# A hybrid decoder block on one core: mixing-gate chunks dealt 2, 2, 2, 10, a third bank for spread decays, routing over 65 candidates with six gather slots

## The chip, the cores and the metric

One Trainium2 chip, one of its cores, one launch. The metric is the device time of the launch in microseconds. The engines are named as in the profile: PE (TensorE, matmul; PEld is its weight load), DVE (VectorE), ACT (ScalarE), POOL (GpSimd) and SP (SyncE, which here only issues DMAs).

## The reference, cut to what matters

512 tokens, width 1024, with 16 meta tokens ahead (528 columns, TOK). One layer:

```python
xn = rms_norm(h, g1); proj = xn @ w_in     # sb q,k,v | dn q,k,v | dn z | b, a | gate_sb, gate_dn
o_sb = stick_breaking_attention(rms_norm(q), rms_norm(k), v)          # 8 heads of 64
o_dn = gated_delta_rule_chunked(l2(silu(conv(dq))), l2(silu(conv(dk))), silu(conv(dv)), beta, g)
o_dn = rms_norm(o_dn) * silu(z)
mix = sigmoid(gate_sb) * (o_sb @ w_sb_out) + sigmoid(gate_dn) * (o_dn @ w_dn_out)
h = h + mix @ w_o
# PEER: 8 heads, 2 x 128 sub keys, top 16 of each half, then top 16 of the 16 x 16 sums
s1, i1 = lax.top_k(s[:, :, 0], 16); s2, i2 = lax.top_k(s[:, :, 1], 16)
cand_s = s1[..., :, None] + s2[..., None, :]
cand_i = i1[..., :, None] * 128 + i2[..., None, :]
top_s, pos = lax.top_k(cand_s, 16); expert_idx = cand_i[pos]; gate = softmax(top_s)
y[t] = sum_e gelu(x[t] . u_tab[expert_idx]) * gate * v_tab[expert_idx]
h = h + y
```

## The kernel before, in words

The kernel has two halves, `front` and `back`. Every float32 product with a large weight is made of three matmuls on a high and a low part (`products`, lines 84 to 86): ACT copies out the high part (`hi`), DVE or POOL subtracts it to get the low one (`lo`, `low`).

**front** computes the projections and both branches, for four pairs of heads one after the other. Its weights come as 40 chunks of 128 columns through a ring of three (`ring`). A chunk is eight steps of TensorE, one for each 128 rows of the contraction: a step of a gate, z or q chunk is three matmuls of 512 columns, one of a k, dq, dk or dv chunk six of 264. Six chunks belong to each pair; the 16 chunks of the two mixing gates (`gate`) belong to none and are dealt out by `GATES_PER_PAIR`, so many to each pair. `Plan` spreads the steps over named places of a pair's program (`room`: "start", "sums", "grow1", "sums2", "grow2" to "grow4", "turned", ("kk", n), "inverse0", ("level", a), ("unit", u), "wt", ("chain", n, s), "end"); a pair's quota is its share of the gates and then the six chunks of the next pair. It also says where a chunk's weights are split and its result taken (`split`, `take`), at most a place or so behind the steps. The projections of pair i+1 so run among the attention and delta-rule work of pair i.

Early in a pair stands the spreading of the decays. For each of five token tiles n (tile 0 is the 16 meta tokens) `grow(n)` on TensorE copies rows of log-decays and betas over all partitions into a PSUM bank (line 1019); DVE's `grow_rows(n)` reads it (800), ACT takes exponentials (592, 595), DVE's `beta_decay(n)` multiplies (808), and POOL masks (439). The banks are `n % 2`, so that `grow(n)` from n = 2 on waits for `beta_decay(n - 2)`. Then come ten transposes (1042 to 1045) into banks 4, 2 and 5, the k k^T products (1053), the blockwise inverse (1063 to 1096), in whose places the attention runs (1107 to 1130), and a chain over the tiles (1139 to 1179) with a norm at its end (1185).

**back** mixes, projects out, makes queries and scores, and then streams the experts: 128 chunks of `activations(j)` (24 matmuls of 384 columns, 3 for each 128 rows) and 128 of `outputs(j)`. In the activations ACT runs `hi(U + s)`, then at set places `exponents(i)` (line 1436, which first waits for DVE's `shifted`), then `gelu(s - 3)`; `activations(j)` waits for `gelu(j - 2)` and for the low part of its own chunk, which POOL makes (line 1520) for j = 3 to PAIRS_A + 2 and DVE after that.

Meanwhile DVE routes (`route(i)`, four tiles of 128 tokens): top 16 of each half, by `best` (MAX8, FIND_INDEX8 and MATCH_REPLACE8), the 16 x 16 sums (line 1672), top 16 of 256 sums in each of 8 heads, and, by comparing positions with 0 to 15 (1688), multiplying (1692) and summing (1697), the two sub keys of each pick. `turn(i)` and `take` bring a tile's picks to columns at chunks ROUTED_AT. The first 128 tokens (FEW) are computed in another way: POOL gathers their experts' rows, one row of 1024 for each token (line 1514), in 128 gathers of u and 128 of v, and DVE multiplies them (`few_next`, "dots", 1721 and 1728). POOL's first R = 4 gathers stand ahead of `low(U + 13)`; after that `sent` grows with j. 78 dots (26 a tile) go with the routing of tiles 1 to 3 in a ring of four slots (`few_ring`), 50 with the gates in two slots (`u_ring`), the v rows in `few_ring` again. `u_ring` shares its memory with the later `w_hi` and `w_lo`, `few_ring` with the one-hot tiles.

From chunk PAIRS_A on, 48 `gates(p)` (two-hot matmuls) follow the activations of one chunk each. The last DVE work ahead of the outputs is the trailing dots and lows. SP loads weights and stores activations in program order (`load_next`, line 1341, waits for the low part of the chunk ahead; `store_acts`, 1349), and after all 128 it loads back what the outputs need (`load_w`, 1360 and 1363); then DVE `weigh`s (1756).

## Time and profile before

| | |
|---|---|
| median of three runs | 2131.11 us (2120.71, 2133.23, 2131.11) |
| the profiled execution's own time | 2122.74 us |
| its span, first to last instruction | 2121.0 us |
| busy: PE, PEld, DVE, ACT, POOL | 1971.5, 1751.7, 1392.6, 815.3, 674.7 us |
| mean of a high part on ACT (1401), a low part on POOL (1520) | 1061 ns, 2575 ns |
| front, to the last norm (line 1185) | 0 to 689 us |
| activations | 901 to 1547 us |
| outputs | 1555 to 2117 us |

The span is one profiled execution, from its first to its last instruction. Busy time counts only what an engine computes. A wait list says for whom an engine waited; in a timeline a row's second number is its duration, and the bracket is the idle time ahead of it with what ended it. A granted clock of 1.00 is 2.4 GHz.

### The profile page before, as it was taken

To read this page: it belongs to the slowest core of one execution; us is meant where nothing else is said; L and a number is where in the kernel's file an instruction comes from. 1 tells how busy PE (TensorE), PEld (TensorE's weight loads), DVE (VectorE), ACT (ScalarE), POOL (GpSimd) and SP (SyncE) were. 2 spreads that over 40 slices of the span, in tenths; PEclk is the share of its full clock that TensorE was granted. 3 is DMA by queue.
4 is the path that set the end of the run, shared out by engine and by line. 5 is a ranking of instruction groups with operands and counts; after the bars stand their busy time and mean duration, and the time that the engine had idled before them with its cause. 6 is when DMAs were issued, how large, how long until landed. Compare 5 with 4: busy or idle time off the path is not lost. (4 is left out here: it accounts for less than half of the span.)

```text
span 2121.0 us, 30502 instructions
## 1 busy us (share of the span) xinstructions
PE 1971.5 (93%) x11569; PEld 1751.7 (83%) x11569; DVE 1392.6 (66%) x2636; ACT 815.3 (38%) x1260; POOL 674.7 (32%) x685
## 2 busy tenths in 40 slices
PE   8889989899898799989999989989989999999999
PEld 7767676676665588889898989989989999999999
DVE  5543443443542564399898968788767777777777
ACT  4333433433433443233333336655523333333332
POOL 4133033033031100058979761222312223222221
PEclk9999999999999899999999999999999999999999
DMA  3210110210210652248888877888889999999997
GB/s 113 85 40 21 55 41 21 69 37 11 70 36 6 225 157 82 80 125 294 289 308 300 296 248 259 323 303 310 304 283 323 325 319 324 326 321 328 325 328 243
DMA packets 153377, 421.75 MB, mean 199 GB/s; under 512 B 15760, under 2 KB 69136, under 8 KB 152592
## 3 DMA queue, kind: packets, MB, share of 16 engines
q1 hardware_dynamic: 114448, 279.27, 38.0%
q0 software_dynamic: 38784, 140.53, 20.0%
q8 instruction: 93, 1.52, 0.3%
q14 instruction: 52, 0.43, 0.1%
HBM read 365.21 MB, written 54.53 MB: 198 GB/s over the span
## 5 line engine op out<-in xcount | busy, mean ns | idle before, releaser
L1401 ACT ACTIVATE expert_hi<-raw 128x1024 fp32r<-128x1024 f32 x288 | 305.4, 1061 | 429.1 <-PE psE L86 394.3
L84 PE MATMUL psE<-x2h,expert_hi 128*128 128x384 f32 x1024 | 353.3, 345 | 28.5 <-POOL expert_lo L1520 20.2
L84 PE MATMUL psE<-w_hi,expert_hi 128*128 128x384 f32 x1024 | 350.7, 342 | 16.4 <-DVE expert_lo L1556 7.5
L1556 DVE TENSOR_TENSOR expert_lo<-raw,expert_hi 128x1024 fp32r<-128x1024 f32 x212 | 259.5, 1225 | 148.7 <-ACT expert_hi L1401 147.8
L86 PE MATMUL psE<-x2h,expert_lo 128*128 128x384 f32 x1024 | 346.9, 339 | 0.0
L85 PE MATMUL psE<-x2l,expert_hi 128*128 128x384 f32 x1024 | 346.8, 339 | 0.0
L86 PE MATMUL psE<-w_hi,expert_lo 128*128 128x384 f32 x1024 | 343.8, 336 | 0.0
L85 PE MATMUL psE<-w_lo,expert_hi 128*128 128x384 f32 x1024 | 343.6, 336 | 0.0
L1514 POOL DMA_INDIRECT few_gathered<-in_peer_v,picked_expert x128 | 135.7, 1060 | 431.1 <-DVE shared L1728 389.7
L1520 POOL TENSOR_TENSOR expert_lo<-raw,expert_hi 128x1024 fp32r<-128x1024 f32 x76 | 195.7, 2575 | 144.5 <-ACT expert_hi L1401 142.9
L84 PEld LDWEIGHTS psE<-w_hi,expert_hi 128*128 128x128 f32 x1024 | 192.6, 188 | 38.3 <-issue 28.0
L84 PEld LDWEIGHTS psE<-x2h,expert_hi 128*128 128x128 f32 x1024 | 196.3, 192 | 33.4 <-POOL expert_lo L1520 24.6
L85 PEld LDWEIGHTS psE<-x2l,expert_hi 128*128 128x128 f32 x1024 | 196.1, 192 | 0.0
L86 PEld LDWEIGHTS psE<-x2h,expert_lo 128*128 128x128 f32 x1024 | 195.7, 191 | 0.0
L85 PEld LDWEIGHTS psE<-w_lo,expert_hi 128*128 128x128 f32 x1024 | 192.8, 188 | 0.0
L86 PEld LDWEIGHTS psE<-w_hi,expert_lo 128*128 128x128 f32 x1024 | 192.7, 188 | 0.0
L1432 ACT ACTIVATE gelu<-psE 128x384 f32<-128x384 f32 x128 | 63.0, 492 | 318.1 <-PE psE L86 318.0
L84 PE MATMUL psB<-xh,ring_h 128*128 128x264 f32 (+1 forms) x448 | 169.0, 377 | 16.2 <-DVE proj L675 12.1
L1728 DVE SCALAR_TENSOR_TENSOR shared<-few_gathered,few_act,shared 128x1024 f32<-128x1024 f32 x127 | 162.5, 1279 | 0.3
L85 PE MATMUL psB<-xl,ring_h 128*128 128x264 f32 (+1 forms) x448 | 152.6, 341 | 0.0
L86 PE MATMUL psB<-xh,ring_l 128*128 128x264 f32 (+1 forms) x448 | 152.0, 339 | 0.0
L881 DVE TENSOR_TENSOR inverse<-inverse,psB 128x512 f32<-128x512 f32 (+3 forms) x108 | 64.1, 594 | 123.8 <-PE psB L1096 123.6
(286 smaller groups left out, 3624.9 us busy)
## 6 DMA issues: line engine op xcount, KB each, us to landing
raw<-in_peer_u SPq DMA_DIRECT2D x128, 512.0 KB, 4.5
raw<-in_peer_v SPq DMA_DIRECT2D x128, 512.0 KB, 6.9
expert_acts<-gelu SPq DMA_DIRECT2D x128, 192.0 KB, 5.1
shared<-expert_acts SPq DMA_DIRECT2D x128, 192.0 KB, 4.0
expert_gates<-shared SPq DMA_DIRECT2D x5, 4096.0 KB, 17.2
shared<-expert_gates SPq DMA_DIRECT2D x32, 640.0 KB, 6.7
ring<-in_w_xonly SPq DMA_DIRECT2D x24, 512.0 KB, 3.4
ring<-in_w_full SPq DMA_DIRECT2D x16, 512.0 KB, 3.8
```

Of the source, the lines that this page charges most:

```text
L84: nc.tensor.matmul(out, sh, mh, start=first, stop=False)
L85: nc.tensor.matmul(out, sh, ml, start=False, stop=False)
L86: return nc.tensor.matmul(out, sl, mh, start=False, stop=last)
L881: inc(nc.vector.tensor_tensor(part, part, bank[0:r, 3 if t % 2 else 5, 0:4 * r].rearrange("p (e w c) -> p e w c", e=2, w=2)[:, :, w0:, :], ...
L1401: nc.scalar.activation(wh[:, s % R, :], raw[:, s % R, :], ACT.Copy).then_inc(S["hi_done"], 1)
L1432: nc.scalar.activation(acts[:, j % R, :], ps[:, 6 + j % 2, 0:MANY], ACT.Gelu).then_inc(S["gelu_done"], 1)
L1514: pool.indirect_dma_start(ring[:, r, :], None, source, bass.IndirectOffsetOnAxis(ap=picked_expert[:, n % HK:n % HK + 1], axis=0)).then_inc ...
L1520: nc.gpsimd.tensor_tensor(wl[:, s % R, :], raw[:, s % R, :], wh[:, s % R, :].bitcast(F32), ALU.subtract).then_inc(S["lo_done"], 1)
L1556: v.tensor_tensor(wl[:, s % R, :], raw[:, s % R, :], wh[:, s % R, :].bitcast(F32), ALU.subtract).then_inc(S["lo_done"], 1)
L1728: last = v.scalar_tensor_tensor(out=few_y, in0=ring[:, r, :], scalar=share, in1=few_y, op0=ALU.mult, op1=ALU.add)
```

## The change

Four things are changed.

1. `GATES_PER_PAIR` is (2, 2, 2, 10) and was (3, 3, 3, 7).
2. `grow(n)` uses banks 0, 1 and 4 in turn and waits for `beta_decay(n - 3)`; the transposes, which write bank 4, wait for `beta_decay` of tile 2.
3. `route` builds 65 sums for each head, in five blocks (`CORNERS`): row 0 with all 16 columns, rows 1 and 2 with 8, 3 to 6 with 4, 7 to 14 with 2, row 15 with 1. A sum that stands in none of them has at least 16 sums that are not smaller. The sub keys are found from a position by 16 start values (`starts`): one comparison (is_ge), a multiplication with the differences of neighbouring rows' index plus start (`corner_step`) and a sum; then by small operations, and by one comparison (is_equal), a multiplication and a sum for the second half.
4. The gathered rows have one ring of 2 + R = 6 slots: all six in the routing, slots 0 and 1 with the gates, 2 to 5 for v. Six gathers stand ahead of `low(U + 13)`. TILE_DOTS is 25 and was 26, ROUTED_AT (13, 33, 53, 73) and was (13, 34, 55, 76), and `exponents(i)` stands one chunk later (s + 3 for s + 4).

```diff
-GATES_PER_PAIR = (3, 3, 3, 7)
+GATES_PER_PAIR = (2, 2, 2, 10)
...
+        def grow_bank(n):
+
+            return (0, 1, 4)[n % 3]
...
-                        decays[0:r, n, :, 0, 0:r], bank[0:r, n % 2, 2 * r:4 * r].rearrange("p (e c) -> p e c", e=2),
+                        decays[0:r, n, :, 0, 0:r], bank[0:r, grow_bank(n), 2 * r:4 * r].rearrange("p (e c) -> p e c", e=2),
...
-                    if n >= 2:
-                        wait("decay_beta", n - 1)
+                    if n >= 3:
+                        wait("decay_beta", n - 2)
...
                 wait("silued", 3)
+                wait("decay_beta", 3)
...
-TILE_DOTS = 26
+TILE_DOTS = 25
...
-ROUTED_AT = (13, 34, 55, 76)
+ROUTED_AT = (13, 33, 53, 73)
+CORNERS = ((0, 1, 16), (1, 2, 8), (3, 4, 4), (7, 8, 2), (15, 1, 1))
+CANDS = sum(a * b for _, a, b in CORNERS)
...
-        def few_seat(n):
...
+        seats, turns, users = [], [0] * (2 + R), {}
+        for n in range(2 * HK):
+
+            r = n % (2 + R) if n < ROUTE_DOTS else (n - ROUTE_DOTS) % 2 if n < FIRST_DOTS else 2 + (n - FIRST_DOTS) % R
+            turns[r] += 1
+            seats.append((r, turns[r], users.get(r, -1) + 1))
+            users[r] = n
...
-                if s + 4 in ROUTED_AT:
-                    exponents(ROUTED_AT.index(s + 4))
+                if s + 3 in ROUTED_AT:
+                    exponents(ROUTED_AT.index(s + 3))
...
-            for n in range(R):
+            for n in range(2 + R):
                 gather(n)
-            sent = R
+            sent = 2 + R
...
-                step(v.tensor_tensor(square(cand), along(val[:, :, 0, :]), across(val[:, :, 1, :]), ALU.add))
+                at_row = 0
+                for a, rows_, cols_ in CORNERS:
+                    part = [P, HEADS, rows_, cols_]
+                    last = v.tensor_tensor(
+                        cand[:, :, at_row:at_row + rows_ * cols_].rearrange("p h (a b) -> p h a b", b=cols_),
+                        val[:, :, 0, a:a + rows_].rearrange("p h (a b) -> p h a b", b=1).broadcast_to(part),
+                        val[:, :, 1, 0:cols_].rearrange("p h (a b) -> p h a b", a=1).broadcast_to(part), ALU.add)
+                    at_row += rows_ * cols_
+                step(last)
...
-                for k in range(2):
-                    last = v.tensor_tensor(square(match[:, k, :, :]), ranks, along(rankf[:, k, :, :]), ALU.is_equal)
-                step(last)
...
+                step(v.tensor_tensor(square(match[:, 0, :, :]), along(posf), small(0), ALU.is_ge))
                 dots_next()
...
+                step(v.tensor_tensor(square(match[:, 0, :, :]), square(match[:, 0, :, :]), across(corner_step),
+                                     ALU.mult))
+                step(v.tensor_reduce(flat(picked[:, 0, :]), square(match[:, 0, :, :]), AX_X, ALU.add))
                 dots_next()
...
+                step(v.tensor_copy(rank[:, 0, :, :], flat(picked[:, 0, :])))
+                step(v.tensor_scalar(rank[:, 1, :, :], rank[:, 0, :, :], KEYS * P - KEYS, None, ALU.bitwise_and))
+                v.tensor_tensor(flat(picked[:, 0, :]), rank[:, 0, :, :], rank[:, 1, :, :], ALU.subtract)
+                step(v.tensor_tensor(posf, posf, rank[:, 1, :, :], ALU.subtract))
+                step(v.tensor_tensor(square(match[:, 1, :, :]), along(posf), small(1), ALU.is_equal))
+                step(v.tensor_tensor(square(match[:, 1, :, :]), square(match[:, 1, :, :]), across(idxf[:, :, 1, :]), ALU.mult))
+                v.tensor_reduce(flat(picked[:, 1, :]), square(match[:, 1, :, :]), AX_X, ALU.add)
                 dots_next()
```

How the steps move on TensorE, in pair 1 and around the spreading: before, nine gate steps stand between the sums of squares and the transposes (4, 3 and 2 of them, three rows each), with a `grow` behind each lot.

```order
L84 MATMUL psB<-xh,ring_h 128x512
L85 MATMUL psB<-xl,ring_h 128x512
L86 MATMUL psB<-xh,ring_l 128x512
...
L1019 MATMUL psB<-rows_in,ones 128x512
L1042 MATMUL psB<-ident,kq 128x128
```

Now one gate step (the last that this pair has), `grow(2)` and `grow(3)` in a row, three steps of the next pair's dq, `grow(4)`, and three dq steps more.

```order
L1016 MATMUL psB<-norm_work,blocks 128x16
L84 MATMUL psB<-xh,ring_h 128x512
L85 MATMUL psB<-xl,ring_h 128x512
L86 MATMUL psB<-xh,ring_l 128x512
L1023 MATMUL psB<-rows_in,ones 128x512 x2
L84 MATMUL psB<-xh,ring_h 128x264
L85 MATMUL psB<-xl,ring_h 128x264
L86 MATMUL psB<-xh,ring_l 128x264
...
L1023 MATMUL psB<-rows_in,ones 128x512
...
L1047 MATMUL psB<-ident,kq 128x128
```

In the whole of such a pair, 2 dq steps (6 before) follow the transposes, then 0, 2, 2, 2, 2 (2, 0, 2, 2, 2 before) the five k k^T products, and none (2) the first transposes of the inverse; from there on nothing is changed in pairs 0 to 2. In pair 3 the counts up to the third cumulated attention tile are as before, and 24 gate steps more stand behind it, at the places of the levels, "unit", "wt" and the first "chain", where pairs 0 to 2 have 24 steps of z, k and q and pair 3 had none.

On POOL, at the head of the activations, before the low part of chunk 13:

```order
L1520 TENSOR_TENSOR expert_lo<-raw,expert_hi 128x1024 x10
L1514 DMA few_gathered<-in_peer_u_rows,picked_expert 128x1024 x4
L1520 TENSOR_TENSOR expert_lo<-raw,expert_hi 128x1024
L1514 DMA few_gathered<-in_peer_u_rows,picked_expert 128x1024
```

and now:

```order
L1524 TENSOR_TENSOR expert_lo<-raw,expert_hi 128x1024 x10
L1518 DMA few_gathered<-in_peer_u_rows,picked_expert 128x1024 x6
L1524 TENSOR_TENSOR expert_lo<-raw,expert_hi 128x1024 x3
L1518 DMA few_gathered<-in_peer_u_rows,picked_expert 128x1024
```

The six gathers stand ahead of chunk 13's low part, and the next one behind three low parts.

On DVE, at the end of the activations, before: the last one-hot tiles, a dot, a low part, four dots, and then the last low part of the activations and two of the outputs.

```order
L1747 TENSOR_TENSOR second_lo<-second_hot,hot_cols 128x1024
L1721 SCALAR_TENSOR_TENSOR u_gathered,few_act<-u_gathered,psE 128x1024
L1556 TENSOR_TENSOR expert_lo<-raw,expert_hi 128x1024
L1721 SCALAR_TENSOR_TENSOR u_gathered,few_act<-u_gathered,psE 128x1024 x4
L1556 TENSOR_TENSOR expert_lo<-raw,expert_hi 128x1024 x3
L1756 TENSOR_TENSOR shared<-shared 128x320
```

and now, with the gates three chunks earlier, seven dots are spread over four low parts:

```order
L1770 TENSOR_TENSOR second_lo<-second_hot,hot_cols 128x1024
L1744 SCALAR_TENSOR_TENSOR few_gathered,few_act<-few_gathered,psE 128x1024
L1560 TENSOR_TENSOR expert_lo<-raw,expert_hi 128x1024
L1744 SCALAR_TENSOR_TENSOR few_gathered,few_act<-few_gathered,psE 128x1024
L1560 TENSOR_TENSOR expert_lo<-raw,expert_hi 128x1024
L1744 SCALAR_TENSOR_TENSOR few_gathered,few_act<-few_gathered,psE 128x1024 x2
L1560 TENSOR_TENSOR expert_lo<-raw,expert_hi 128x1024
...
L1560 TENSOR_TENSOR expert_lo<-raw,expert_hi 128x1024 x3
L1779 TENSOR_TENSOR shared<-shared 128x320
```

Three chunks of the activations now lie between the last gates and the outputs that were not there before.

## Rows read from the trace of the kernel before

**Rows 1.** Windows: us, engines' busy us (instructions), granted clock, DMA share, GB/s.
```profile
241.00:244.00 3.00, 3.00 (x14) 2.43 (x14) 2.82 (x5) 1.84 (x3) 0.00 (x0) 1.00 0.00 0
260.40:263.90 3.50, 3.50 (x10) 2.59 (x9) 1.54 (x4) 0.96 (x3) 0.41 (x1) 0.56 0.00 0
967.40:1257.10 289.70, 271.12 (x1520) 267.04 (x1521) 260.97 (x775) 98.46 (x133) 247.25 (x139) 0.98 0.89 298
1140.00:1199.00 59.00, 59.00 (x343) 58.97 (x342) 52.12 (x191) 20.19 (x28) 49.63 (x31) 1.00 0.94 333
```

**Rows 2.** Timeline, TensorE, pairs 1 and 3: start, us, operation, [idle before <-releaser].
```profile
254.71 0.29 PE L1012 MATMUL psB<-norm_work,blocks 128*128 128x16 f32 x2
259.81 1.15 PE L1019 MATMUL psB<-rows_in,ones 128*128 128x512 f32 x2 [1.93 <-DVE decays L808]
269.71 1.13 PE L1019 MATMUL psB<-rows_in,ones 128*128 128x512 f32 x2 [2.88 <-DVE decays L808]
318.65 0.81 PE L1121 MATMUL psB<-conv_work,negones 128*128 128x384 f32 x2
391.91 0.70 PE L1185 MATMUL psB<-norm_work,blocks 128*128 128x512 f32 x1 [1.45 <-ACT norm_work L648]
562.14 0.29 PE L1012 MATMUL psB<-norm_work,blocks 128*128 128x16 f32 x2
581.78 0.27 PE L1042 MATMUL psB<-ident,kq 128*128 128x128 f32 x1
628.85 0.81 PE L1121 MATMUL psB<-conv_work,negones 128*128 128x384 f32 x2
688.95 1.12 PE L1185 MATMUL psB<-norm_work,blocks 128*128 128x512 f32 x2 [1.46 <-ACT norm_work L648]
```

**Rows 3.** VectorE's groups by shape, 880:1262: count, busy us, mean ns, idle.
```profile
L1635 DVE MAX8 shared<-shared 128x8 f32<-128x128 f32 x128 | 25.5, 278 | 0.8 <-ACT shared L1425 0.7
L1635 DVE MAX8 shared<-shared 128x8 f32<-128x256 f32 x64 | 21.7, 410 | 0.1
L1639 DVE FIND_INDEX8 half_index<-shared 128x8 uint32<-128x128 f32 x128 | 33.6, 284 | 0.0
L1639 DVE FIND_INDEX8 top_position<-shared 128x8 uint32<-128x256 f32 x64 | 25.4, 419 | 0.0
L1672 DVE TENSOR_TENSOR shared<-shared 128x2048 f32<-128x2048 f32 x4 | 9.1, 2278 | 0.0
L1688 DVE TENSOR_TENSOR shared<-iotaf,shared 128x2048 f32<-128x2048 f32 x8 | 22.8, 2889 | 0.0
```

**Rows 4.** Timeline of several engines at the first tile's routing.
```profile
940.56 0.31 ACT L1436 ACTIVATE shared<-shared 128x128 f32<-128x128 f32 x1 [11.24 <-DVE shared L1681]
942.82 0.66 PE L84 MATMUL psE<-x2h,expert_hi 128*128 128x384 f32 x1 [7.95 <-ACT gelu L1432]
960.20 1.01 POOL L1514 DMA_INDIRECT few_gathered<-in_peer_u_rows,picked_expert  x1 [3.75 <-DVE picked_gate L1711]
967.40 0.44 PE L84 MATMUL psE<-x2h,expert_hi 128*128 128x384 f32 x1 [1.69 <-POOL expert_lo L1520]
```

**Rows 5.** Waits, 968:1240: us in total, times, longest.
```profile
POOL few_gathered L1514 <- DVE few_gathered L1721: 25.0, 15, 3.9
```

**Rows 6.** Timeline of VectorE and GpSimd in the second tile's routing.
```profile
1022.62 6.09 DVE L1688 TENSOR_TENSOR shared<-iotaf,shared 128x2048 f32<-128x2048 f32 x2
1024.50 2.82 POOL L1514 DMA_INDIRECT few_gathered<-in_peer_u_rows,picked_expert  x1 [0.16 <-issue]
```

**Rows 7.** Timeline at the turn from activations to outputs.
```profile
1543.89 0.60 SPq L1360 DMA_DIRECT2D shared<-expert_acts  x1
1552.06 0.49 DVE L1756 TENSOR_TENSOR shared<-shared 128x320 f32<-128x320 f32 x1 [6.86 <-issue]
1554.93 0.66 PE L84 MATMUL psE<-w_hi,expert_hi 128*128 128x384 f32 x1 [7.51 <-DVE expert_lo L1556]
```

**Rows 8.** The page's DMA issues: KB each, median us to landing.
```profile
raw<-in_peer_u SPq DMA_DIRECT2D x128, 512.0 KB, 4.5
```

More of the change, by code:

```diff
@@ L591, in _ @@
                             h = slice(e * HD, (e + 1) * HD)
-                            last = nc.scalar.activation(egr[h, n, :], bank[h, n % 2, e * P:(e + 1) * P], ACT.Exp)
+                            last = nc.scalar.activation(egr[h, n, :], bank[h, grow_bank(n), e * P:(e + 1) * P], ACT.Exp)
                         inc(last, "row_exp")
@@ L798, in grow_rows @@
                     for e in range(2):
-                        last = nc.vector.tensor_scalar(decays[0:r, n, e, 1, 0:r], bank[0:r, n % 2, e * r:(e + 1) * r],
+                        last = nc.vector.tensor_scalar(decays[0:r, n, e, 1, 0:r], bank[0:r, grow_bank(n), e * r:(e + 1) * r],
                                                        scalars[0:r, 2, n, 2 * i + e:2 * i + e + 1], 0.0,
@@ L1270, in carve @@
             return view
[L1272 removed]
+        cand = carve([HEADS, CANDS])
         match = carve([2, HEADS, TOPK * TOPK])
@@ L1683, in route @@
                 dve.wait_ge(S["shifted"], i + 1)
-                step(v.tensor_copy(rankf, rank[:, :, :, :]))
+                v.tensor_scalar(posf, pos[:, :, :], float(KEYS), None, ALU.mult)
+                step(v.tensor_tensor(corner[:, :, 1:], idxf[:, :, 0, :], starts[:, 0:1, :].broadcast_to([P, HEADS, TOPK]),
+                                     ALU.add))
+                step(v.tensor_tensor(corner_step, corner[:, :, 1:], corner[:, :, 0:TOPK], ALU.subtract))
                 dots_next()
-                ranks = c["iotaf"][:, :].rearrange("p (h a b) -> p h a b", h=1, a=1).broadcast_to(grid)
@@ L1787, in _ @@
             dve.wait_ge(S["score_stored"], 2 * HEADS)
+            v.tensor_scalar(starts[:, 1, :], c["iotaf"][:, :], float(KEYS), None, ALU.mult)
+            step(v.tensor_scalar(starts[:, 0, :], c["iotaf"][:, :], 1.0, None, ALU.add))
+            step(v.tensor_scalar(corner_bits[:, :], starts[:, 0, :].bitcast(U32), 19, None, ALU.logical_shift_right))
+            step(v.tensor_scalar(starts[:, 0, :], corner_bits[:, :], 127.0 * 16, float(KEYS), ALU.subtract, ALU.mult))
             for i in range(NT):
```

53 lines of the change are left out of this document (21 added, 32 removed).

## The prediction

> **What bounds the kernel now.** I read the page first: TensorE is busy for 1971.5 of 2121 us, far ahead of DVE, so time can only come from TensorE's own pauses and from stretches at its lower clock. None of the four edits removes matmuls: they are moved. So I went through TensorE's timeline for pauses, and at each asked who released it. Three kinds concern this change.
>
> In the front a full-speed matmul of 512 columns starts every 0.23 us (some 13 in 3.00 us) [rows 1], so a step costs 0.70 us. In pair 1, TensorE waits twice in the spreading of the decays for `beta_decay`, 1.93 and 2.88 us [rows 2]. Behind the first the granted clock is 0.56, near the 1.2 GHz level, and ten matmuls take 3.50 us [rows 1]: 0.35 to 0.45 each, so a pause of 2 us costs about as much again.
>
> In the activations a chunk is 24 matmuls. Where nothing disturbs (1140 to 1199 us) 343 take 59.00 us [rows 1], that is 0.172 each and 4.15 a chunk. The 63 chunks from 967.40 to 1257.10 took 289.70 us where 63 x 4.15 is 261.5: 28 us lost, of which 18.6 are TensorE idle and the rest slow clock [rows 1]. TensorE waits there for POOL's low parts. POOL in turn waited 25.0 us in this stretch for DVE to free a gather slot [rows 5], and it is held up while DVE compares two SBUF operands: a gather takes 2.82 us beside line 1688 and 1.01 alone [rows 6, 4].
>
> Two single pauses: 7.95 us ahead of chunk 8, for a `gelu` that stood behind `exponents(0)` on ACT, which itself had waited 11.24 us for DVE's routing; and 7.51 us ahead of the first outputs [rows 4, 7].
>
> **Part 1, pairs 0 to 2 lose a gate chunk each.** Pure work: 8 x 0.70 = 5.6 us a pair. The pauses beside it: from 254.71 to the last `grow` at 269.71 pass 15.0 us with nine steps and two grows [rows 2]. After, `beta_decay` of tile 0 is no earlier (it hangs on norms and a weight split on DVE, all unmoved): the bank wait of tile 2 goes, but tile 3 waits for the same event, at about 259.7. Then a grow (0.5), three dq steps at the low clock (3.9), and the last `grow` stands at some 264.3: 5.4 us earlier, though two gate steps' cover is bare (a pause of 3.4 us now, where 1.93 was). DVE has tile 1's and 2's product done by then, so the added wait ahead of the transposes is covered by the three dq steps. Behind the last `grow` 13 steps are left of 16 (2.2 us), and about 1 us of slow clock goes with the second pause. Against it: only two dq steps (1.5 us) hide the 2.5 us in which DVE makes the scaled k and v, 1 us bare. Sum 5.4 + 2.2 + 1 - 1 = 7.6, with the steps ahead of the inverse gone where TensorE waited anyway about 8.5. Three pairs: **-25** (-17, the work alone, to -28).
>
> **Pair 3 gets 24 steps.** The trace shows this exact stretch with and without such steps: from 318.65 to 391.91 in pair 1 (25 steps) 73.3 us, from 628.85 to 688.95 in pair 3 (one step) 60.1 [rows 2]. So 24 steps cost 13.2 and not 24 x 0.70 = 16.8: **+13** (up to +17).
>
> **Part 2, the third bank in pair 3**, where the steps between the grows stay: 562.14 to 581.78 is 19.6 us [rows 2], 13 steps (9.1) and three grows (1.5) are 10.6, plus 1 for switching. Nothing else should be late: tile 0's product is ready at about 567, `grow(3)` comes at 568, and DVE needs some 2 us a tile. **-8** (-4, its two waits alone, to -8.5). Front: -20.
>
> **Part 3, routing on DVE.** MAX8 takes 25.5/128 = 0.199 us on 128 values and 21.7/64 = 0.339 on 256; FIND_INDEX8 0.262 and 0.397 [rows 3]. Straight lines give 0.13 and 0.19 at 65, neither measured there. Sixteen of each and eight MATCH_REPLACE8 (priced like FIND_INDEX8) save 3.3 + 3.3 + 1.6 = 8.2 us a tile; one sum of 2.28 us [rows 3] becomes five short ones (about 1.2). Position arithmetic and waits between its steps add some 2. Net 7 us, and a dot of 1.3 fewer. DVE does not bound TensorE, so this pays only through what it releases.
>
> In tile 0 `shifted` comes 9 us earlier, at about 932, and ACT asks for it a chunk later, at 932: the 7.95 us pause goes, and with it about 2 us of slow clock, as after the pause in rows 1. But POOL waits for the picks before the low part of chunk 13, now behind six gathers for four. The picks come at 959.9 less 9 plus 3 of new small steps, 954. From the first gather at 960.20 to TensorE's restart at 967.40 four gathers and a low part took 7.2 us [rows 4]; with 2.4 for the low part a gather is 1.2, so six and the low part end at 954.2 + 9.6, at 963.8. TensorE, 10 us earlier, wants chunk 13 at 955.6. So it stops there for 8 us, where it stopped for 1.69 [rows 4], and pays the slow clock again. What is left is **-2** (-12 if the four locked operations run free and the picks come at 949 with the slow clock spared; +4 if not).
>
> **Part 4, six slots.** The 25.0 us of POOL's slot waits [rows 5] should nearly go, and chunks 13 and 14 bring no gather, so POOL starts 2.5 us richer. A chunk costs POOL 2.4 + 1.25 x 1.1 = 3.8 us of TensorE's 4.15; it gains 0.35 a chunk, 7 a tile, and the four wide two-operand operations take about 6 from it as they did. That balances: **-22** of the 28 (-9 to -27). The turn from gates to outputs: DVE's last low part of the activations stood behind four dots in a row; now three chunks more lie between the last gates and the outputs, and I get SP's first load back about 8 us earlier against TensorE. Before, 11.0 us passed between it at 1543.89 and the outputs [rows 7]. **-8** of 7.51 and its slow clock (-3 to -9). Gates, their five pauses (at each 4 MB store) and the outputs: 0, plus or minus 3.
>
> **The port.** Rows 6 show a gather nearly three times as long beside a DVE comparison, and line 1688 at 2889 ns on average where the same size takes 2278 at line 1672 [rows 3]. The Trainium skill ("SBUF — State Buffer", Who interferes with whom) says that DVE and GpSimd share a port pair as an exclusive lock, that a DVE instruction with two SBUF inputs holds off a GpSimd one that reads SBUF, and infers that it leaves descriptor generation alone. The lock agrees with the trace; that gathers go free does not, by 1.8 us. It speaks against this change: the same four wide operations remain and now start singly, each able to catch POOL anew. That is the first rival.
>
> **Sum.** -25 + 13 - 8 - 2 - 22 - 8 = -52. The profiled execution's own time is 2122.74, so 2071. It is 8 us under the median of the runs, 2131.11; the same 2.4% off that median gives 2079. I put the forecast between, at 2074.
>
> **Rivals.**
> - *POOL stays the limit.* The lock, not the slots, makes TensorE's waits: part 4 gives -9 and chunk 13 +4. Sum -33, 2093. For: the gather of 2.82 us. Against: slot waits of 25.0 are as large as the whole loss. If the short searches have a fixed cost that 65 values do not lower, it ends here too. Chance 0.19.
> - *The front's pauses are a chain of DVE and ACT*, and removed steps only bare them: -17 + 17 - 4 = -4. Sum -36, 2090. Against: pair 1 and pair 3 differ by less than their steps. Chance 0.10; both together 2109, 0.05.
> - *Everything hidden goes*: -28 + 12 - 8.5 - 12 - 27 - 9 = -72, 2054. Chance 0.06.
> - *Slower: weight loads starve behind six gathers.* Place: the activations of the routing. A raw tile is free after its low part; load, high part (1.06) and low part (2.6 on the page) must fit in four chunks, 16.6 us, so the landing may take up to 12.9; it takes 4.5 at the median [rows 8]. The load is 333 GB/s in the clean stretch [rows 1], near the highest the page shows, so two more 512 KB gathers in flight could lengthen it. At 18 us a chunk takes 5.4: +75 on 60 chunks, less front and turn (-28), +47, 2170. Against: `sent` fixes the rate, not the slots. Chance 0.03.
> - The forecast 0.57.
>
> **Range.** From 2054 to 2098: it leaves out the slower case, both rivals together and little else. A measurement of this kernel can tell about 1%, 21 us. Faster by over 1% are all cases but the slow one and half of the 2109: 0.93; within 1% 0.04; slower 0.03.
>
> **What would show it.** Pairs 0 to 2 145 us each (153.7), the sums' `grow(2)` with no wait, one wait of over 3 us at `grow(3)`; pair 3 about 5 us longer; no wait for `gelu` at chunk 8, one of 8 us for POOL at chunk 13; almost no other waits for POOL's low parts; MAX8 at 65 values 0.13 us; the first outputs without a wait. I am wrong if chunk 13 stays as cheap as before (a better time), if POOL's low parts still stop TensorE in each tile, or if the landing of raw tiles passes 10 us.

## The result: 1.3% faster, half of what was forecast

The changed kernel takes 2100.86 us in the median (2087.82 to 2104.40, four runs) beside 2126.99 (2120.71 to 2133.23) for the kernel before: ratio 0.9866, 95% interval 0.9819 to 0.9912. The forecast was 2074, and 2054 to 2098 its range. The profiled execution is the quickest of the four, 2087.82 us with a span of 2086.1. A second profile of the same kernel (`e16_changed_again` below), span 2101.2, is nearer to the others, and what tells the two apart is part of the answer.

The front first. TensorE's timeline in pair 1, and the norms that end pairs 1 and 3, answer to [rows 2]:

```profile
250.00 0.29 PE L1016 MATMUL psB<-norm_work,blocks 128*128 128x16 f32 x2
250.93 1.02 PE L1023 MATMUL psB<-rows_in,ones 128*128 128x512 f32 x2
255.10 2.04 PE L1023 MATMUL psB<-rows_in,ones 128*128 128x512 f32 x2 [3.16 <-DVE decays L812]
259.86 1.02 PE L1023 MATMUL psB<-rows_in,ones 128*128 128x512 f32 x2
266.52 0.85 PE L1058 MATMUL psB<-kq 64*16 64x16 f32 x8 [0.90 <-DVE v_beta L849]
280.31 2.08 PE L1068 MATMUL psB<-ident,inverse 16*16 16x16 f32 x10 [1.80 <-DVE inverse L873]
383.74 1.13 PE L1190 MATMUL psB<-norm_work,blocks 128*128 128x512 f32 x2 [1.46 <-ACT norm_work L652]
679.92 1.12 PE L1190 MATMUL psB<-norm_work,blocks 128*128 128x512 f32 x2 [1.45 <-ACT norm_work L652]
```

The window of pair 1, with the columns of [rows 1], and its part from the last `grow` on:

```profile
233.54:383.74 150.20, 137.47 (x817) 102.51 (x817) 62.49 (x118) 57.83 (x122) 37.27 (x72) 0.95 0.12 36
259.86:383.74 123.88, 114.30 (x731) 86.59 (x729) 44.46 (x82) 39.65 (x88) 36.26 (x69) 0.96 0.09 29
```

The same part in the kernel before:

```profile
269.71:391.91 122.20, 113.79 (x746) 86.67 (x746) 45.57 (x83) 39.60 (x88) 36.66 (x70) 0.99 0.10 32
```

The third bank works: `grow(2)` at 250.93 has no wait, and the one ahead of `grow(3)` is 3.16 us, as the forecast drew it. From the sums to the last `grow` pass 9.9 us for 15.0, 5.1 less where 5.4 was forecast. But behind it the pair takes 1.7 us longer than before and not 2.2 less: idle time is 1.2 us more, and busy time does not fall though 15 matmuls are gone, as the granted clock is 0.96 for 0.99; the whole pair takes 150.2 us where 145 was forecast and 153.7 stood before. The front ends at 679.9, 9 us earlier than in [rows 2] and not 20.

Then the back, by the same engine's timeline:

```profile
953.59 0.69 PE L84 MATMUL psE<-x2h,expert_hi 128*128 128x384 f32 x1 [6.70 <-POOL expert_lo L1524]
1216.21 0.90 PE L1930 MATMUL psE<-ident,shared 128*128 128x128 f32 x3 [5.74 <-DVE shared L1727]
1221.04 0.26 PE L1943 MATMUL psE<-second_hi,first_hot 128*128 128x128 f16 x1 [3.93 <-DVE second_lo L1770]
1508.66 0.45 PE L84 MATMUL psE<-x2h,expert_hi 128*128 128x384 f32 x1 [2.42 <-DVE expert_lo L1560]
1519.78 0.66 PE L84 MATMUL psE<-w_hi,expert_hi 128*128 128x384 f32 x1 [6.66 <-DVE expert_lo L1560]
```

And two windows: tiles 1 to 3, to be held against 967.4 to 1257.1 in [rows 1], and the last tile alone.

```profile
953.60:1206.20 252.60, 252.60 (x1447) 252.53 (x1448) 244.10 (x771) 93.73 (x127) 232.71 (x131) 0.99 0.94 321
1110.00:1216.00 106.00, 100.47 (x581) 100.12 (x579) 105.00 (x283) 37.98 (x52) 91.41 (x51) 0.99 0.88 295
```

The wait for `gelu` at chunk 8 [rows 4] is gone and the one at chunk 13 is there, as forecast. In the tiles TensorE does not stop at all in this execution. Two things were not forecast: the turn of the last picks waits 5.74 us for VectorE (line 1727), and the wait ahead of the first outputs, 7.51 us in [rows 7], is still 6.66 with a new one of 2.42 ahead of chunk 127. The last window shows the first of these from VectorE's side: 105.0 us busy of 106. POOL's slot waits of [rows 5] fell to this, over 968 to 1216 (6.5 us of it up to the last turn, and the longest one behind it):

```profile
POOL few_gathered L1518 <- DVE few_gathered L1744: 10.6, 12, 4.1
```

The searches of [rows 3], and the groups of the new steps behind them:

```profile
L1639 DVE MAX8 shared<-shared 128x8 f32<-128x65 f32 x64 | 8.9, 213 | 0.1
L1643 DVE FIND_INDEX8 top_position<-shared 128x8 uint32<-128x65 f32 x64 | 12.7, 219 | 0.0
L1714 DVE CAST half_rank<-shared 128x128 uint32<-128x128 f32 x4 | 5.4, 1354 | 0.0
L1718 DVE TENSOR_TENSOR shared<-shared,corner_start 128x2048 f32<-128x2048 f32 x4 | 11.2, 2812 | 0.1
L1719 DVE TENSOR_TENSOR shared<-shared 128x2048 f32<-128x2048 f32 x4 | 13.3, 3333 | 0.1
```

MAX8 takes 8.9/64 = 0.139 us at 65 values, FIND_INDEX8 0.198: the straight lines of the forecast held. The cast of line 1714 did not. VectorE's timeline shows why, once in tile 0, where the cast falls between two of POOL's low parts and POOL is idle at the reduction, and once in tile 3, where POOL makes low parts all along:

```profile
932.36 0.23 DVE L1714 CAST half_rank<-shared 128x128 uint32<-128x128 f32 x1
940.14 2.29 DVE L1720 TENSOR_REDUCE shared<-shared 128x128 f32<-128x2048 f32 x1
...
1190.68 2.68 DVE L1714 CAST half_rank<-shared 128x128 uint32<-128x128 f32 x1
1193.39 2.43 DVE L1715 TENSOR_SCALAR half_rank<-half_rank 128x128 uint32<-128x128 uint32 x1
1195.85 2.51 DVE L1716 TENSOR_TENSOR shared<-half_rank 128x128 f32<-128x128 uint32 x1
1198.60 4.37 DVE L1718 TENSOR_TENSOR shared<-shared,corner_start 128x2048 f32<-128x2048 f32 x1
1203.00 4.37 DVE L1719 TENSOR_TENSOR shared<-shared 128x2048 f32<-128x2048 f32 x1
1207.40 2.29 DVE L1720 TENSOR_REDUCE shared<-shared 128x128 f32<-128x2048 f32 x1
...
1190.85 18.77 POOL L1524 TENSOR_TENSOR expert_lo<-raw,expert_hi 128x1024 fp32r<-128x1024 f32 x6
```

A cast of 128 values takes 0.23 us between two low parts and 2.68 when six of them run back to back on POOL; one low part takes 2.55 us in the mean. The three small operations take 7.6 us together, the two wide ones 4.37 each where [rows 3] have 2.28 for one; the reduction is 2.29 in both tiles. The Trainium skill ("SBUF — State Buffer", Who interferes with whom) says that casts and `tensor_scalar` can take the port pair that DVE shares with GpSimd, that whoever comes first blocks the other for a whole instruction, and that a reduction never does. The rows agree with each of the three.

### The profile page after: what moved, and what is told of

The parts are those of the page before. It is cut to its first block and busy times, and to the rows that moved or that the text cites. A ratio compares the mean times of both kernels' runs of the same rounds, so it can differ in the third digit from the quotient of the medians.

```text
span 2086.1 us, 30537 instructions
## 1 busy us (share of the span) xinstructions
PE 1964.2 (94%) x11569; PEld 1748.2 (84%) x11569; DVE 1385.8 (66%) x2676; ACT 815.2 (39%) x1260; POOL 661.6 (32%) x682
## 5 line engine op out<-in xcount | busy, mean ns | idle before, releaser
L1518 POOL DMA_INDIRECT few_gathered<-in_peer_u_rows,picked_expert x128 | 154.6, 1207 | 251.5 <-DVE few_gathered L1744 225.3
L1524 POOL TENSOR_TENSOR expert_lo<-raw,expert_hi 128x1024 fp32r<-128x1024 f32 x73 | 186.3, 2552 | 132.9 <-ACT expert_hi L1405 131.2
L1744 DVE SCALAR_TENSOR_TENSOR few_gathered<-few_gathered,psE 128x1024 f32<-128x1024 f32 x128 | 153.7, 1217 | 53.6 <-DMA few_gathered<-in_peer_u_rows,picked_expert 52.3
```

What stands on the lines that cost most here:

```text
L1518: pool.indirect_dma_start(few_ring[:, r, :], None, source, bass.IndirectOffsetOnAxis(ap=picked_expert[:, n % HK:n % HK + 1], axis=0)).then ...
L1524: nc.gpsimd.tensor_tensor(wl[:, s % R, :], raw[:, s % R, :], wh[:, s % R, :].bitcast(F32), ALU.subtract).then_inc(S["lo_done"], 1)
L1744: last = v.scalar_tensor_tensor(out=rows_of, in0=rows_of, scalar=1.0, in1=rows_x, op0=ALU.mult, op1=ALU.mult, accum_out=share)
```

## The experiments

"Last norm" is the start of the last norm product of the front (line 1185 or 1190).

The kernels e1 to e4, e5 to e8, e9 to e12 and e13 to e16 shared a chip each with the kernel before, whose medians there were 2121.45, 2122.81, 2123.78 and 2121.99.

| kernel | median us | ratio, 95% interval | span of the profile |
|---|---|---|---|
| e1_front_alone | 2115.02 | 0.9972 (0.9956 to 0.9988) | 2113.9 |
| e2_third_bank_alone | 2102.39 | 0.9907 (0.9871 to 0.9944) | 2100.4 |
| e3_dealing_alone | 2134.37 | 1.0061 (1.0039 to 1.0083) | 2129.7 |
| e4_routing_alone | 2104.91 | 0.9919 (0.9891 to 0.9947) | 2094.0 |
| e5_dealing_as_before | 2090.55 | 0.9848 (0.9825 to 0.9871) | 2088.4 |
| e6_lows_before_picks | 2100.37 | 0.9888 (0.9863 to 0.9913) | 2102.9 |
| e7_last_turn_at_75 | 2077.32 | 0.9794 (0.9767 to 0.9822) | 2074.9 |
| e8_lows_before_dots | 2090.88 | 0.9861 (0.9817 to 0.9905) | 2087.9 |
| e9_dots_between | 2090.37 | 0.9832 (0.9807 to 0.9856) | 2088.3 |
| e10_second_gathers_later | 2080.41 | 0.9779 (0.9748 to 0.9809) | 2080.8 |
| e11_together | 2077.95 | 0.9776 (0.9750 to 0.9801) | 2083.0 |
| e12_together_early_lows | 2091.89 | 0.9838 (0.9807 to 0.9868) | 2089.0 |
| e13_turns_as_before | 2078.09 | 0.9790 (0.9766 to 0.9815) | 2077.1 |
| e14_last_gathers_in_six | 2072.44 | 0.9771 (0.9743 to 0.9798) | 2070.8 |
| e15_four_slots | 2086.94 | 0.9829 (0.9805 to 0.9854) | 2085.6 |
| e16_changed_again | 2099.94 | 0.9881 (0.9851 to 0.9911) | 2101.2 |

### The front: dealing and bank, each alone

`e1_front_alone` is the kernel before with the diff's first two parts; `e2_third_bank_alone` has the bank without the first line below, `e3_dealing_alone` only that line; `e4_routing_alone` has the rest of the change and neither.

```diff
-GATES_PER_PAIR = (3, 3, 3, 7)
+GATES_PER_PAIR = (2, 2, 2, 10)
```

e1: 

> The kernel before with the dealing 2, 2, 2, 10 and the third bank alone. My theory: the front brings what the trace of the changed kernel shows up to its last norm, 9 us (688.95 to about 680), and nothing behind it moves: 9 us faster, ratio 0.996. The rival is my forecast: the front brings 20 us by itself (last norm at 669, ratio 0.990), and what was missing in the changed kernel came from elsewhere.

e2: 

> The kernel before with the third bank alone, steps dealt 3, 3, 3, 7. My theory: the bank brings its 8 us in pair 3, where its cover stays, and in pairs 0 to 2 about 1 us each, since the wait moves to the third tile's spreading and the scaled k and v behind it: last norm at 678, 11 us faster, so the dealing by itself is worth nothing or costs 2 us. The rival, by which the dealing brings 12 us (25 less 13) and the bank 8: last norm at 681 at best here and 669 with both.

e3: 

> The kernel before with the dealing 2, 2, 2, 10 alone, two banks. My theory: pairs 0 to 2 get 3 us shorter each, since removed steps bare waits for VectorE, and pair 3 some 11 to 13 longer: last norm at 691, 2 us later than before. The rival (removed steps bring their work and their share of waits): 25 less 13, last norm at 677, 12 us earlier.

e4: 

> The changed kernel with the front as before (3, 3, 3, 7 and two banks): routing over 65 candidates, six slots and turns at chunks 13, 33, 53 and 73 alone. My theory: the front at 689 as before, and behind it the 26 us that the two traces differ by from the activations on: span about 2095, ratio 0.988. The rival, by which the two halves are not additive (another state of the clock or of the memory): more than 5 us away from that, to either side.

The last norm came at 682.8 with both, at 670.8 with the bank alone and at 702.2 with the dealing alone, against 689.0 before. The bank brings 18 us, more than the 11 expected, the dealing costs 12 with the bank and 13 without, where I had expected 2, and the medians say the same (19 us less, 13 more, 6 less). The routing alone brings 17 us by the medians; its profile has 27, and like the first profile of the changed kernel it has no wait in tile 2 (below). Pair 1 as a window, with both:

```profile
234.74:384.97 150.23, 137.50 (x816) 102.55 (x816) 62.50 (x118) 57.82 (x122) 37.23 (x72) 0.95 0.11 36
```

And with the bank alone:

```profile
233.73:381.33 147.60, 137.07 (x840) 102.36 (x840) 64.74 (x120) 58.68 (x123) 37.26 (x72) 1.00 0.13 42
```

These are the rows to learn from: 24 matmuls of 512 columns fewer, and TensorE is as long busy (137.50 and 137.07), because the clock fell from 1.00 to 0.95; idle time rose from 10.5 to 12.7. The removed steps had filled the waits for VectorE in the first third of the pair: from the sums to the last `grow` pass 8.2 us with them, at a clock of 1.00, and 9.7 without, at 0.82. With them gone the clock of the four windows of 10 us from 254.7 to 294.7 is 0.83, 0.83, 0.93 and 0.73; with the bank alone it is 1.00 in all of the pair. The 5.6 us of work came back as 2.2 us of idle time and, by an estimate from the busy times, 6 of slow clock. This pair is the clearest of them: over the twelve profiles with the bank and 3, 3, 3, 7 pair 1 takes 147.6 to 150.7 us at a clock of 1.00 to 0.98, over the three with the bank and 2, 2, 2, 10 it takes 150.2 to 151.9 at 0.95 to 0.94. Pair 2 ends at 529.6 to 534.8 in the twelve and at 534.0 to 536.9 in the three.

### The changed kernel with the front put right

`e5_dealing_as_before` is the changed kernel with 3, 3, 3, 7, and the base of all that follow.

> The changed kernel with the steps dealt 3, 3, 3, 7 as before, everything else as changed. My theory, from the third bank alone and the dealing alone: the dealing costs 12 us in this kernel too, so the last norm comes at 671 instead of 680 or a little over 9 us earlier and the span is some 2075, ratio to the kernel before 0.979. The rival (the dealing's cost and the routing's gain are not additive): span 2083 to 2087.

The median is 10 us under the changed kernel's (2090.55 to 2100.86, on other chips; the ratios to the kernel before are 0.985 and 0.987, and 0.988 for e16, with intervals that overlap), and the last norm came at 671.6; over the twelve profiles of this front it comes between 665.1 and 674.0, over the three with 2, 2, 2, 10 and the bank at 679.9, 682.3 and 682.8. But the span of 2088 was nearer the rival's than mine: 9 us were lost in tile 2, 8 of them at a wait of 6.1 us ahead of chunk 52, that the first profile of the changed kernel does not have. (The expectations below call it the wait ahead of chunk 51; counted from 0 as chunk 13 is, it is the one behind chunk 51.)

`e16_changed_again` is the changed kernel once more, `e9_dots_between` (on e5) moves two groups of dots into the stretch where it happens:

```diff
                 step(v.tensor_tensor(posf, posf, rank[:, 1, :, :], ALU.subtract))
+                dots_next()
                 step(v.tensor_tensor(square(match[:, 1, :, :]), along(posf), small(1), ALU.is_equal))
+                dots_next()
...
                 step(v.tensor_reduce(total[:, :], gate, AX_X, ALU.add))
-                dots_next()
-                dots_next()
```

e16: 

> The changed kernel itself once more, to see its other executions: if its profiled execution was one without the wait at chunk 51, this one has a wait of about 6 us there in half of the cases or more, and its median stands 8 us above the 2088 of that execution, at 2096 to 2104; if chunk 51 is clean here too, the spread of its runs has another place.

e9: 

> As the dealing 3, 3, 3, 7, with two of the last three groups of dots of a tile moved up: one ahead of the comparison of the second half's corners, one behind it, so that no 13 us pass on VectorE without a dot. The kernel with that dealing showed POOL waiting 8.54 us for a slot in this stretch and TensorE 6.11 us ahead of chunk 51, about 8 us in all, which the profiled execution of the changed kernel did not show. If the stretch without a dot makes it, the wait is gone: 8 us less, median about 2083, and the wait for the last picks of 5.8 us stays within 1 us. The rival: POOL is late because wide operations with two operands lock it out, and then TensorE still stops by 4 us or more at one of the chunks 50 to 53 or 68 to 73.

The changed kernel has the wait too when its span is 2101. TensorE, POOL and VectorE there (`e16_changed_again`):

```profile
1128.18 0.69 PE L84 MATMUL psE<-x2h,expert_hi 128*128 128x384 f32 x1 [6.20 <-POOL expert_lo L1524]
...
1124.80 0.94 POOL L1518 DMA_INDIRECT few_gathered<-in_peer_u_rows,picked_expert  x1 [8.54 <-DVE few_gathered L1744]
...
1110.13 2.68 DVE L1714 CAST half_rank<-shared 128x128 uint32<-128x128 f32 x1
1113.38 3.03 DVE L1717 TENSOR_TENSOR shared<-shared,half_rank 128x128 f32<-128x128 f32 x1
1116.45 2.29 DVE L1718 TENSOR_TENSOR shared<-shared,corner_start 128x2048 f32<-128x2048 f32 x1
1118.78 2.29 DVE L1719 TENSOR_TENSOR shared<-shared 128x2048 f32<-128x2048 f32 x1
1121.11 2.29 DVE L1720 TENSOR_REDUCE shared<-shared 128x128 f32<-128x2048 f32 x1
1123.31 1.21 DVE L1744 SCALAR_TENSOR_TENSOR few_gathered<-few_gathered,psE 128x1024 f32<-128x1024 f32 x1
```

From 1110.1 to 1123.3 the new position arithmetic runs without a dot, so no slot comes free; POOL stands 8.54 us at a gather, the low part of chunk 52 stands behind it, and TensorE stops, 8.5 us with the slow clock in chunks 51 and 52 (10.5 and 6.3 for 4.15 each). In the first profile of the changed kernel a slot was free when POOL asked: VectorE begins this arithmetic 144.1 us after the start of chunk 13 there and 153.4 us after it here. The lag begins at a dot that waits 3.44 us for its row and not 1.58, and grows at small operations that fall beside a low part in one execution and not in the other. In e9 this wait was gone, as expected of the stretch, and the time came back as 1.56 and 2.16 us ahead of chunks 52 and 53 and 4.04 ahead of chunk 69: the rival's sign, and no gain. The wait at the last turn went with them, since TensorE came later. So the stretch places the wait, but does not make it.

### What makes it: the slots or the pace

`e15_four_slots` takes the six slots back in the tiles, with four gathers ahead of chunk 13; `e13_turns_as_before` gives the tiles 21 chunks again; `e7_last_turn_at_75` gives only the last one more, 22. In both the gathers are thinned in all tiles, as POOL deals the 75 out over the chunks up to the last turn: 75 over 60 chunks in e5, over 62 in e7, over 63 in e13.

```diff
-            r = n % (2 + R) if n < ROUTE_DOTS else ...
+            r = n % R if n < ROUTE_DOTS else ...
...
-ROUTED_AT = (13, 33, 53, 73)
+ROUTED_AT = (13, 34, 55, 76)
```

e15: 

> As the dealing 3, 3, 3, 7, with four slots for the gathers of the tiles instead of six and four of them ahead of chunk 13. My prediction's view (the slots made POOL late): waits for POOL come back in each of tiles 1 to 3, 15 us or more, less 3 us at chunk 13, median 2100 or more. The rival (the shorter routing on VectorE freed the slots soon enough, six were not needed): within 4 us of the same kernel with six, 2087 to 2094.

e13: 

> As the dealing 3, 3, 3, 7, with the turns at chunks 13, 34, 55 and 76 as before: routing over 65 candidates and six slots with 21 chunks a tile. If the pace of 20 chunks a tile leaves VectorE and POOL no time, both waits go, the 6.1 us ahead of chunk 51 and the 5.8 us ahead of the turn, in all some 13 us with the slow clock, against 2 to 5 us lost at the turn to the outputs, where one low part is left for seven dots: median about 2080. The rival, by which the stretch without a dot makes the wait at any pace: a wait of over 4 us for POOL stays in the second or third tile, median 2088 or more.

e7: 

> As the dealing 3, 3, 3, 7, and the last turn of picks, with the first gates behind it, at chunk 75 instead of 73. If VectorE's lateness with the last tile (picks at 1215.9 where TensorE wanted them at 1210.5) makes the wait of 5.7 us, it is gone, and the turn costs as before, about 11 to 12 us in its chunk instead of 16.5: 5 us less there. The gates then end two chunks later and I expect the turn to the outputs unchanged or up to 2 us longer. The rival: VectorE falls further behind with more chunks beside it (POOL's low parts lock it out for longer), and the wait stays at 3 us or more.

Four slots are no slower than six: 2086.9 and 2090.5 (ratios 0.983 and 0.985, with intervals that overlap). They have more waits for POOL in the tiles (12, 13.6 us in all, beside 2 of 6.8 us in `e16_changed_again`), but wait less at chunk 13 (4.42 us) and not at the last turn, as TensorE comes there later. POOL's waits for a slot from chunk 13 to the last turn, with four slots at 20 chunks (`e15_four_slots`):

```profile
POOL few_gathered L1518 <- DVE few_gathered L1744: 20.2, 19, 3.4
```

With six at 20 (`e16_changed_again`):

```profile
POOL few_gathered L1518 <- DVE few_gathered L1744: 20.7, 14, 8.5
```

With six at 21 (`e13_turns_as_before`):

```profile
POOL few_gathered L1518 <- DVE few_gathered L1744: 0.6, 3, 0.3
```

At 21 chunks the waits vanish, and with them TensorE's ahead of chunk 52 and at the last turn. From the start of chunk 0 to that of chunk 80 pass 372.3 us with four slots, 371.7 with six (e5), 370.7 with the dots between, 361.9 and 372.3 in the two profiles of the changed kernel, but 354.9 with the last turn at 75 and 353.1 at 76 (of which 2 and 3 us are gates that come later). More slots do not shorten this; they only move the place of the wait.

What does is not only the number of chunks, for the first two tiles of e7 have 20 as in e5. Tile 2 in e5:

```profile
1030.90:1122.80 91.90, 85.79 (x485) 85.43 (x485) 90.97 (x268) 31.82 (x43) 73.99 (x46) 0.96 0.87 298
```

And in e7:

```profile
1025.00:1108.50 83.50, 83.50 (x485) 83.46 (x484) 82.61 (x258) 31.70 (x43) 76.64 (x45) 1.00 0.94 326
```

VectorE is busy 99% in both, and TensorE does not stop in the second. So a full VectorE is not enough to stop it; in that tile the two kernels differ only in how densely POOL gathers. With four slots VectorE is busy 88% over tiles 2 and 3 and TensorE waits all the same. What the runs suggest is that VectorE and POOL together have next to no reserve at 20 chunks and 75 gathers in 60: VectorE's arithmetic of the last tile begins 235.9 us after chunk 13 with the turn at 75 or 236.0 at 76, and 246.5 in e5. The wait ahead of chunk 52 stands in four of the six profiles with 75 gathers in 60 chunks and unmoved dots (e5, e8, e10, e16, and not in e4 and the first one), and in none of the three with 75 in 62 (e7, e11, e14; e12, with its early low parts, aside). For the last tile, which of the two brings the gain, thinner gathers or a later turn, was not tried.

The later turn has its price: with one low part left for seven dots (turn at 76) TensorE waits 11.6 us ahead of chunk 127, and at 75 the chunks 126, 127 and the first of the outputs take 27.9 us, 5 more than in e5 where I had expected 2.

`e6_lows_before_picks` attacks the wait at chunk 13:

```diff
-            for j in range(3, ROUTED_AT[0]):
+            for j in range(3, ROUTED_AT[0] + 3):
                 low(U + j)
             pool.wait_ge(S["few_picked"], 2)
```

> As the dealing 3, 3, 3, 7, and POOL makes the low parts of chunks 13, 14 and 15 before it waits for the picks, which it does behind chunk 12 otherwise. If the 6.7 us in front of chunk 13 and the slow clock behind it come from POOL's order alone, both go: chunks 12 and 13 take 4.2 us each instead of 11 and 7, 9 us less. The rival: the low parts run beside VectorE's wide operations with two operands and hold up the picks, so the first gathers and then chunk 16 or 17 come 3 to 4 us late and half of it is lost again.

Chunks 12 and 13 took 4.2 us each, and chunks 16 to 32 lost 19: the same 8.54 us wait of POOL, now in tile 1 as well as ahead of chunk 52. The stop at chunk 13 had given POOL and VectorE 9 us to catch up, which is the likely reason. It was 10 us slower; even the rival had only half of the gain lost.

### The turn to the outputs

`e8_lows_before_dots` puts each group of the seven dots behind the gates after its low part (the first lines below); `e10_second_gathers_later` adds to that a wait on POOL ahead of the gathers of v rows; `e11_together` takes the turn at 75 and the dots between to it, `e12_together_early_lows` e6's edit as well; `e14_last_gathers_in_six` is e11 without the dots between and with the last u gathers spread.

```diff
+                low(U + N - rest + k)
                 for _ in range(k * trailing // rest, (k + 1) * trailing // rest):
                     few_next()
-                low(U + N - rest + k)
...
+            pool.wait_ge(S["weighted"], 2)
             for n in range(FIRST_DOTS, 2 * HK):
                 gather(n)
...
+            if FIRST_DOTS - 5 <= n < FIRST_DOTS - 1:
+                r = 2 + n - (FIRST_DOTS - 5)
...
             for n in range(ROUTE_DOTS, FIRST_DOTS):
+                if n == FIRST_DOTS - 5:
+                    pool.wait_ge(S["gates_made"], 2 * PAIRS_B)
                 gather(n)
```

e8: 

> As the dealing 3, 3, 3, 7, and of the seven dots behind the gates each group stands behind its chunk's low part on VectorE instead of ahead of it. If the dots' waits for gathered rows (13 us over seven dots) hold up the last low part, and with it the queue of loads and the first outputs, then the wait ahead of chunk 127 (2.4 us) goes and the first outputs come 3 to 5 us earlier. The rival: the first outputs hang on the last dots themselves and on the stores of gates, not on the low part: under 1 us.

e10: 

> As the dealing 3, 3, 3, 7, the low parts ahead of the dots behind the gates, and the first four gathers of v rows wait until two chunks of activations are weighted. With the low parts first alone, the first load of activations was issued 6.3 us earlier and yet landed 12.4 us later instead of 6, while the memory moved 400 GB/s with four gathers of 512 KB in it, and nothing was won. If these gathers take the bandwidth, the load lands some 5 us sooner, the wait of 8.93 us ahead of the first outputs falls to about 4, and the turn (chunks 126, 127 and the first of the outputs, 23 to 24 us) takes 18 to 19. The rival: the stores of gates and activations or the last gathers of u rows take it, and it stays over 22.

e11: 

> The dealing 3, 3, 3, 7, the last turn at chunk 75, the dots between, the low parts ahead of the dots and the gathers of v rows later. If the effects add: from the kernel with the turn at 75 (span 2074.9, which had no wait at chunk 51) 5 to 9 us less at the turn to the outputs, span 2066 to 2070, ratio 0.974. If the dots between make the gathers stand differently and bring back waits for POOL, 2075 or more.

e12: 

> As the one before, and POOL makes the low parts of chunks 13 to 15 before it waits for the picks. With the dealing alone this moved the 9 us of chunks 12 and 13 to chunks 16 to 32 and made them 19, since POOL then ran into the stretch without a dot 8 us earlier. If that stretch was the reason, about 6 us are won here against the kernel before; if POOL simply lacks the time for its gathers without the stop at chunk 13, the time moves again and nothing or less is won.

e14: 

> The dealing 3, 3, 3, 7, the last turn at chunk 75, the low parts ahead of the last dots, the gathers of v rows later, and of the last seven gathers of u rows four go to slots 2 to 5 once the gates are made. In the kernel without this the last dot ran at 1504.1, 8 us behind its last load, with the memory idle, and the first outputs waited 11.2 us. If the two slots make that, the last dots end 6 to 8 us earlier and the first outputs wait 3 to 5 us: span about 2068, ratio 0.972, the fastest here. The rival: the first load of activations, behind the stores of gates, ends last anyway, and 2 us or less are won.

Chunks 126, 127 and the first of the outputs took 22.9 us in e5 and 23.8 in e8. My theory of the low part fell there: SP issued its first load back at 1503.25, 15.8 us ahead of the outputs where it had been 10.2 in the changed kernel, and nothing was won. SP's loads of activations and gates from 1485 to 1520, by the view of their tile, in e8:

```profile
DMA to landing us min/median/max: 4.4/11.8/12.4
```

In e10:

```profile
DMA to landing us min/median/max: 3.4/6.2/7.8
```

With the four gathers of v rows out of the way the landing takes half as long, and the turn 19.6 us: what the gathers moved was in the way. e11 missed its span (2083.0 for 2066 to 2070), though no wait for POOL came back in the tiles: with the turn at 75 the last dots end last instead. VectorE and TensorE's first outputs in e11:

```profile
1496.77 1.22 DVE L1745 SCALAR_TENSOR_TENSOR few_gathered<-few_gathered,psE 128x1024 f32<-128x1024 f32 x1 [4.46 <-DMA few_gathered<-in_peer_u_rows,picked_expert]
1504.13 1.22 DVE L1745 SCALAR_TENSOR_TENSOR few_gathered<-few_gathered,psE 128x1024 f32<-128x1024 f32 x1 [3.33 <-DMA few_gathered<-in_peer_u_rows,picked_expert]
...
1510.41 0.66 PE L84 MATMUL psE<-w_hi,expert_hi 128*128 128x384 f32 x1 [11.21 <-DVE w_lo L1786]
```

TensorE's first outputs in e14:

```profile
1498.02 0.41 PE L84 MATMUL psE<-w_hi,expert_hi 128*128 128x384 f32 x1 [1.11 <-DVE expert_lo L1564]
```

With four of these gathers in slots 2 to 5 the wait falls from 11.21 to 1.11 us (e14 also leaves out the dots between, which stand in the tiles); 5.0 us come back ahead of the third output chunk, where VectorE waits for the load of gates. e14 is the fastest kernel here: 27.5 us, or 1.3%, under the changed one on the same chip. e12 was 14 us slower than e11 and confirms e6: early low parts only move the wait into the tiles, also with dots in the stretch.

## Why the prediction was wrong

By its own steps, with the terms in us; "typical" is the second profile (2101.2), since three of the four first runs took as long.

- **Pairs 0 to 2, -25: the step that failed.** The term held the effect of both edits, and together they brought 9 to 12 us (pair 2 ends at 536.9, 536.5 and 534.0 for 545.6). Taken apart, all of it is the bank's: the dealing cost 3 us (without the bank) to 5 (with it). Up to the last `grow` the working held (5.1 us of 5.4 in pair 1). It failed behind it, at "13 steps are left of 16 (2.2 us), and about 1 us of slow clock goes with the second pause": 1.7 us more passed there than before, 1.2 of them idle, and the clock fell to 0.96 from 0.99. "Pure work: 8 x 0.70 = 5.6 us a pair" counted removed matmuls as time; they were the cover of waits, and in pair 1 of e1 beside e2 their 5.6 us went into 2.2 of idle time and 6 of slow clock.
- **Pair 3, 24 steps, +13**: 10.5 without and 6.9 with the bank (5 to 10 against the twelve profiles with the bank and the old dealing); the sign right, the size off, since there the steps fill waits (idle time 4.4 us in e1 for 9.4 in e2) and the clock is 1.00 for 0.96.
- **Third bank, -8**: right in pair 3 with the new dealing, which was forecast (7.9; the stretch that was worked out as 11.6 us took 11.9); with the old dealing e2 has 4.3 of it left at the pair's end, at a clock of 0.95 behind the last `grow`, and the twelve profiles have 3 to 8. It brings 11 to 14 us more in pairs 0 to 2, which the forecast had mixed into the first term. Together the front brought 6 to 9 us instead of 20.
- **Tile 0, -2**: held. The gelu pause went, the stop at chunk 13 came: 6.70 us with chunks 12 and 13 at 11.0 and 6.4 us, 9 lost where 8 and the slow clock stood. The picks came at 943 and not 954, but TensorE wanted the chunk as much earlier.
- **Tiles 1 to 3, -22**: of the 28 us lost before, 25 are gone in the first profile (60 chunks in 252.6 us, 249 undisturbed) and 15 in the typical one (956.7 to 1219.0), which loses 8.5 ahead of chunk 52 and in it, and 0.7 ahead of chunk 69. The 25 of the first profile is luck beside the others, and the mechanism was wrong: in the medians six slots are worth nothing at this pace (e15). At 21 chunks a tile they may be worth something; that was not tried with four. The first rival (POOL stays the limit, 0.19) is nearest to what the runs showed, though VectorE and POOL hold each other up.
- **"DVE does not bound TensorE"** was the sentence behind this and behind the turns, and it fails in the last tile: 5.74 us at the new turn; chunk 73 and the next take 23.1 us in the typical profile where 17.2 went before. No term of the sum stood for it.
- **Turn to the outputs, -8**: +1 to +2. I took SP's early load for the limit; it was the v gathers' bandwidth and, behind it, u gathers two at a time (e8, e10, e14).
- The gates' pauses and the outputs, 0 plus or minus 3: held (outputs 565.5 us against 566.1 before, in the typical profile).

The typical span stands 20 us under the one before, where 52 were forecast. The 32 missing are 13 in the front, 7 in the tiles, 6 at the last turn and 9 at the outputs, less 3, of which the stretch up to chunk 13 did 2 better than its term and the gates 1. What stays open: why VectorE is 9 us later at the arithmetic of tile 2 in some executions than in others. The traces show where the lag begins and grows, not what starts it.

## What to carry to other kernels

Before you move filler work out of a stretch, price the waits that it covers, at the low clock: read busy time and granted clock of the stretch together, for busy time that stays equal with less work is the sign. Where two edits of a change touch the same waits, each must be tried alone; here the better half of the front was hidden by the worse. And an engine that is busy 66% of the whole, as VectorE here, may be at 99% in the one stretch that is to be shortened: take the busy share of each engine per window before you shorten it. That share counts time for which it is held up (4.37 us for an operation of 2.29), so it warns but does not prove a limit; run the kernel twice, and thin out the producer before you buy it slots.

## Unexpected in the hardware

- A cast, a `tensor_scalar` or a subtraction of 128 values a partition takes DVE 0.2 to 0.3 us alone and 2.2 to 3.0 when it runs into one of POOL's low parts (2.55 in the mean): a small operation can lose a whole POOL instruction.
- Loads of 192 KB (two of 640 among them) landed 11.8 us after their issue at the median with four gathers of 512 KB issued right behind the first (e8), and 6.2 us without (e10).
- The stop at chunk 13 was worth keeping: without it the kernel was 10 us slower in e6 and 14 in e12, as the waits came back larger in the tiles.
